# Norms taken per pair of tiles inside the stage that makes x, with roots out of PSUM, hand-over per tile and feed-forwards written out

## The reference

```python
def rmsnorm(x, g):
    return x * rsqrt(mean(x * x, axis=-1) + 1e-6) * g

# first block, layers l = 0, 1
h = rmsnorm(x, norm_mix[l]) * (1 + scale) + shift          # norm n1
proj = h @ w_in[l]                                         # then RWKV-7 and MLA branches, gates, merged
x = x + gate * (merged @ w_o[l])
h = rmsnorm(x, norm_ffn[l]) * (1 + scale) + shift          # norm n2
f = swiglu(h) if l == 0 else moe_swiglu(h)                 # (silu(h @ w1) * (h @ w3)) @ w2; 8 experts, top 2
x = x + gate * f
x = rmsnorm(x, norm_final)                                 # norm nf

# second block, layers l = 0, 1
h = rmsnorm(x, attn_norm[l])                               # norm m1
proj = h @ w_in[l]                                         # two attentions (q and k normed per head), gates
x = x + merged @ w_out[l]
h = rmsnorm(x, ffn_norm[l])                                # norm m2
x = x + (silu(h @ w1) * (h @ w3)) @ w2
```

## Time and profile before

| | us |
|---|---|
| median of 3 runs | 3870.16 (3866.35 to 3871.33) |
| profiled execution, its time | 3868.01 |
| its span | 3866.2 |
| PE busy | 3623.4 (94%) |
| DVE busy | 817.5 (21%) |
| ACT busy | 466.5 (12%) |
| granted TensorE clock, mean | 0.957 of full speed |

### The profile page before, as it was taken

The page is one execution under the profiler, slowest core; times in us unless marked ns, Lnnn a source line. Parts: engine busy times, 40 slices in busy tenths (PEclk is TensorE's granted clock), DMA queues, the critical chain, the costliest instruction groups (busy, mean ns, idle before and its releaser), DMA issues.

```text
span 3866.2 us, 40342 instructions
## 1 busy us (share of the span) xinstructions
PE 3623.4 (94%) x17522; PEld 2807.9 (73%) x17522; DVE 817.5 (21%) x1610; ACT 466.5 (12%) x1027; POOL 35.8 (1%) x74
## 2 busy tenths in 40 slices
PE   6998799899779999999999999999897899997899
PEld 4886688788557777776566777777685788785788
DVE  3523300362431000000000000000454100454100
ACT  2211200212211000000000000000113000113000
POOL 3000000000000000000000000000000000000000
PEclk8999999999989999999999999999896999996999
DMA  8354244334113444447888998985241344341342
GB/s 273 126 186 143 77 152 152 109 105 144 66 66 109 152 152 153 152 153 246 287 286 301 298 300 297 300 297 163 87 141 33 115 139 158 102 133 33 120 157 93
DMA packets 505396, 633.67 MB, mean 164 GB/s; under 512 B 13674, under 2 KB 458240, under 8 KB 505104
## 3 DMA queue, kind: packets, MB, share of 16 engines
q1 hardware_dynamic: 501392, 626.07, 49.3%
q10 hardware_dynamic: 1440, 3.93, 0.3%
q0 software_dynamic: 2400, 1.26, 0.1%
HBM read 630.17 MB, written 1.05 MB: 163 GB/s over the span
## 4 chain that ended last, share of the span: by engine, by line
PE 90%; DVE 5%; issue 2%; ACT 1%; SPq 1%; DMA 0%; ACTq 0%; DVEq 0%
PE bank L447 62%; PE accum L447 27%; DVE w L1498 1%; SPq L2126 1%; DVE w L1519 1%; DVE w L1504 1%; PE bank L538 1%; PE bank L643 1%; ACT w L1165 0%; DMA ring<-in_ada_w_dram 0%; DVE sh L1519 0%; ACT w L1130 0%; DVE w L1501 0%; ACT L1130 0%; ACT h L1130 0%
## 5 line engine op out<-in xcount | busy, mean ns | idle before, releaser
L447 PE MATMUL bank<-h,ring 128*128 128x256 f32 (+1 forms) x3712 | 813.2, 382 | 26.0 <-issue 26.0
L447 PEld LDWEIGHTS bank<-h,ring 128*128 128x128 f32 (+1 forms) x3712 | 703.8, 191 | 133.7 <-issue 35.8
L447 PE MATMUL bank<-w,ring 128*128 128x256 f32 x2816 | 620.1, 381 | 15.4 <-DVE w L1498 14.4
L447 PEld LDWEIGHTS bank<-w,ring 128*128 128x128 f32 x2816 | 538.1, 191 | 104.9 <-issue 25.8
L447 PE MATMUL bank<-ring,w 128*128 128x256 f32 (+1 forms) x3136 | 598.7, 380 | 0.0
L447 PEld LDWEIGHTS bank<-ring,w 128*128 128x128 f32 (+1 forms) x3136 | 481.0, 175 | 96.9 <-issue 15.2
L1498 DVE TENSOR_TENSOR sg<-bank,sg 128x256 f32<-128x256 f32 x140 | 59.5, 425 | 1380.3 <-ACT sg L1130 1380.3
L447 PE MATMUL accum<-ring,qa 128*128 128x512 f32 (+1 forms) x784 | 303.3, 596 | 0.0
L447 PE MATMUL bank<-w 128*128 128x128 f32 (+7 forms) x1728 | 245.4, 312 | 47.8 <-ACT w L1165 32.4
L447 PEld LDWEIGHTS bank<-w 128*128 128x128 f32 (+3 forms) x1728 | 200.1, 193 | 92.3 <-issue 78.0
L447 PE MATMUL accum<-w,ring 128*128 128x256 f32 x1056 | 231.8, 379 | 0.0
(11 more groups left out here) (247 smaller groups left out, 1913.1 us busy)
## 6 DMA issues: line engine op xcount, KB each, us to landing
ring<-in_moe_w_dram SPq DMA_DIRECT2D x336, 1024.0 KB, 5.1
ring<-in_w_in_dram SPq DMA_DIRECT2D x76, 1024.0 KB, 5.3
ring<-in_ada_w_dram SPq DMA_DIRECT2D x48, 1024.0 KB, 8.3
ring<-in_w_ffn_in_dram SPq DMA_DIRECT2D x44, 1024.0 KB, 5.3
ring<-in_ffn_w_dram SPq DMA_DIRECT2D x33, 1024.0 KB, 5.4
ring<-in_w_ffn_out_dram SPq DMA_DIRECT2D x22, 1024.0 KB, 5.0
ring<-in_w_o_dram SPq DMA_DIRECT2D x8, 1024.0 KB, 5.2
ring<-in_w_out_dram SPq DMA_DIRECT2D x8, 1024.0 KB, 5.2
```

Source lines behind the costliest of these rows:

```text
L447: ins = nc.tensor.matmul(o, lhsT, rhs, start=start, stop=stop, skip_group_check=skip)
```

## The change

- **Pairs.** ACT squares x two tiles at a time (`square_pair`), as soon as DVE has updated both, while the projection (or the last product down, or `combine`) still makes the later tiles. PE adds each pair to the sum at a set place inside that stage (`norm_sums`): behind tiles 2, 4 and 6 of `w_o` and `w_out`, and the fourth pair behind the last tile. The sum of the n2 and m2 norms lies in `accum`.
- **Roots.** ACT reads the sum in PSUM and takes the root of scale times sum plus epsilon in the same instruction (`root`), in all norms, the small ones too; DVE only waits and takes the reciprocal (`inverse_root`). So the banks with sums are drained by ACT, at the place where the root stands in ACT's program.
- **Hand-over.** `full_norm` forms each tile of h in one DVE instruction (x times gain times reciprocal root). Where there is a shift, ACT adds it (`shift_h`). Each tile signals; the first eight products of the next stage wait tile by tile (`normed_h`).
- **Feed-forwards.** No loops: eleven chunks written out on PE, ACT, DVE and SP. The four products with zeros stand behind the first chunk up. The last product down goes tile by tile (`ffn_last`) and signals per two tiles; the closing product is gone. At the very end the output is turned half by half.

```diff
+            def norm_sums(tag, take=take):
+                place = []
+                def pair(p):
+                    if p == 0:
+                        place.extend(take(tag + (0,)))
+                    t, f = place
+                    pe.wait_ge(squared, next_of("squared"))
+                    for k in (2 * p, 2 * p + 1):
+                        ins = mm(t[:, 0:T], ones[:, :], sq[:, k, :], k == 0, k == KD - 1, last=k == KD - 1)
+                    if p == 3:
+                        ins.then_inc(f, 1)
+                return pair
+            def normed_h(k):
+                pe.wait_ge(h_ready, next_of("h_ready"))
+                return h[:, k, :]
...
                         contract(t[:, 0:T], kt, lambda k: w(k, m * P, m * P + P), lambda k: src[:, k, :]).then_inc(f, 1)
+                        if pair and at in (2, 4, 6):
+                            pair(at // 2 - 1)
                     release.append(s)
+                if pair:
+                    pair(3)
...
+            def ffn_last(key, b, pair):
+                s2, w2 = piece(2)
+                for k in range(2):
+                    pe.wait_ge(*read_out(key + (k,)))
+                for m in range(KD):
+                    for k in range(2):
+                        ins = mm(accum[:, m, :], w2(k, m * P, m * P + P), hid[:, b, k, :], False, k == 1,
                                  last=(k == 1 and m == KD - 1), skip=True)
+                    if m % 2:
+                        ins.then_inc(acc_full, one("acc_full"))
+                    if pair and m > 4 and m % 2:
+                        pair(m // 2 - 2)
+                release.append(s2)
+                for p in (2, 3) if pair else ():
+                    pair(p)
+            def ffn(key, pair):
+                n = FF // FW
                 for i in range(n):
+                    ffn_up(key + (i,), i == 0)
+                    for b in range(0 if i else 4):
+                        mm(accum[:, 2 * b:2 * b + 2, :].rearrange("p m t -> p (m t)"), zeros, con[:, 0:512],
+                           True, False, skip=True)
                     if i:
                         ffn_down(key + (i - 1,), (i - 1) % 2)
-                ffn_down(key + (n - 1,), (n - 1) % 2)
+                ffn_last(key + (n - 1,), (n - 1) % 2, pair)
...
                     if m % 2:
                         ins.then_inc(acc_full, one("acc_full"))
+                    if m in (3, 5, 7):
+                        norm(m // 2 - 1)
+                norm(3)
...
+            def square_pair(p):
+                fn(sq[:, 2 * p:2 * p + 2, :], x[:, 2 * p:2 * p + 2, :], ACT.Square).then_inc(squared, one("squared"))
+            def root(keys, buf, n, eps=0):
+                at = 0
+                for key, w in keys:
+                    act.wait_ge(*full(key))
+                    fn(buf[:, at:at + w, :], psum_of(key)[:, 0:w * T].rearrange("p (j t) -> p j t", t=T), ACT.Sqrt,
+                       scale=1.0 / n, bias=c("eps", eps, eps + 1)).then_inc(reader_of(key), 1)
+                    at += w
+            def shift_h(shifts):
+                for j in range(KD):
+                    act.wait_ge(scaled_h, next_of("scaled_h"))
+                    fn(h[:, j, :], h[:, j, :], ACT.Identity, bias=shifts[:, j:j + 1]).then_inc(h_ready, one("h_ready"))
...
-            def norm_scale(key, dst):
-                mean_square([(key, 1)], rs, D, EPS)
-                tt(dst[:, :, :], x[:, :, :], rs[:, 0:1, :].to_broadcast([P, KD, T]), MUL).then_inc(dve_step, 1)
-                dve.wait_ge(dve_step, stepped())
+            def inverse_root(keys, buf, n):
+                for key in keys:
+                    dve.wait_ge(*read_out(key))
+                V.reciprocal(buf[:, 0:n, :], buf[:, 0:n, :]).then_inc(dve_step, 1)
+                dve.wait_ge(dve_step, stepped())
+            def full_norm(key, dst, gains, done, name):
+                inverse_root([key], rs, 1)
                 for j in range(KD):
+                    ins = stt(dst[:, j, :], x[:, j, :], gains[:, j:j + 1], rs[:, 0, :], MUL, MUL)
+                    if done is not x_ready or j % 2:
+                        ins.then_inc(done, one(name))
...
-                tt(x[:, :, :], x[:, :, :], accum[:, :, :], ADD).then_inc(x_ready, one("x_ready"))
+                for p in range(4):
+                    dve.wait_ge(acc_full, next_of("acc_full"))
+                    tt(x[:, 2 * p:2 * p + 2, :], x[:, 2 * p:2 * p + 2, :], accum[:, 2 * p:2 * p + 2, :], ADD
+                       ).then_inc(x_ready, one("x_ready"))
```

More of the change, by code:

```diff
@@ L588, in ffn @@
-            def ffn(key, trips, per, rest):
-                for b in range(4):
-                    mm(accum[:, 2 * b:2 * b + 2, :].rearrange("p m t -> p (m t)"), zeros, con[:, 0:512],
-                       True, False, skip=True)
-                assert not release
-                slots.start(3 * per // SLOTS), banks.start(2 * per // NB)
-                with pe.Fori(0, trips) as i:
-                    reg[0] = i
-                    ffn_steps(key + ("loop",), per)
-                slots.end(trips), banks.end(trips)
-                if rest:
-                    ffn_steps(key + ("rest",), rest)
-                mm(accum[:, 7, :], zeros, con[:, 0:T], False, True, last=True, skip=True).then_inc(acc_full, one("acc_full"))
+                ffn_last(key + (n - 1,), (n - 1) % 2, pair)
@@ L675, in combine, with experts @@
                 return ins
-            def experts():
+            def experts(norm):
                 for a in range(TT):
@@ L744, in _ @@
                 mod_piece(0, 0, q)
-            sumsq(("n1", 0), [range(KD)])
+            first = norm_sums(("n1", 0))
+            for p in range(4):
+                first(p)
             for q in range(8, 12):
@@ L1002, in _ @@
             mm(t[:, 0:4], ones[0:64, :], small[0:64, 0:4], last=True).then_inc(f, 1)
-            pe.wait_ge(x_ready, next_of("x_ready"))
+            first = norm_sums(("m1", 0))
+            for p in range(4):
+                first(p)
+            next_of("x_ready", 4)
             for l in range(2):
@@ L1048, in between @@
                         head_turns(4)
-                sumsq(("m1", l), [range(KD)])
                 nat, gate, u = 0, 0, 0
@@ L1349, in _ @@
                 attention(("mla", l))
-                act.wait_ge(*read_out(("wo", l, 7)))
-                squares(x[:, :, :], 8)
-                root([("n2", l, 0)], rs[:, 0:1, :])
+                for p in range(4):
+                    act.wait_ge(*read_out(("wo", l, 2 * p)))
+                    act.wait_ge(*read_out(("wo", l, 2 * p + 1)))
+                    square_pair(p)
+                root([(("n2", l, 0), 1)], rs, D)
+                shift_h(mod[:, 0:8])
                 if l == 0:
-                    ffn(("ffn", 0), FF // FW // 4, 4, FF // FW % 4)
+                    ffn(("ffn", 0))
                 else:
@@ L1397, in head_roots @@
                     g, n = HN_GROUPS[i]
-                    root([("hn", l, g, j) for j in range((n + 1) // 2)], rs2[:, 0:n, :])
+                    root([(("hn", l, g, j), min(2, n - 2 * j)) for j in range((n + 1) // 2)], rs2, 64)
                 def between(u):
@@ L1472, in _ @@
                 squares(oB2[:, :, :], 4)
-                root([("yb2", l, 0), ("yb2", l, 1)], rs2[:, 0:4, :])
-                act.wait_ge(*read_out(("wo2", l, 7)))
-                squares(x[:, :, :], 8)
-                root([("m2", l, 0)], rs[:, 0:1, :])
-                ffn(("ffn2", l), FF // FW // 4, 4, FF // FW % 4)
-                act.wait_ge(x_ready, next_of("x_ready"))
-            for a in range(TT):
-                for g in range(2):
+                root([(("yb2", l, 0), 2), (("yb2", l, 1), 2)], rs2, P)
+                for p in range(4):
+                    act.wait_ge(*read_out(("wo2", l, 2 * p)))
+                    act.wait_ge(*read_out(("wo2", l, 2 * p + 1)))
+                    square_pair(p)
+                root([(("m2", l, 0), 1)], rs, D)
+                ffn(("ffn2", l))
+                if l == 0:
+                    x_squares()
+            next_of("x_ready", 4)
+            for g in range(2):
+                for a in range(TT):
                     act.wait_ge(*full(("out", a, g)))
@@ L1759, in _ @@
                     modulation(0, 0)
-                    norm_apply(h, gain, mod[:, 0:8]).then_inc(h_ready, one("h_ready"))
                     dve.wait_ge(sines, next_of("sines"))
@@ L2151, in ffn_pieces, with ffn @@
                 down(n - 1)
-            def ffn(w1, w3, w2, trips, per, rest):
-                slots.start(3 * per // SLOTS)
-                with sp_.Fori(0, trips) as i:
-                    reg[0] = i
-                    ffn_pieces(per, lambda q: w1, lambda q: w3, lambda q: w2, lambda q: i * (per * FW) + q * FW)
-                slots.end(trips)
-                if rest:
-                    ffn_pieces(rest, lambda q: w1, lambda q: w3, lambda q: w2, lambda q: (trips * per + q) * FW)
+            def ffn(w1, w3, w2):
```

(1 more changed line is left out.)

195 lines of the change are left out of this document (77 added, 118 removed).

## The result

| | kernel before | changed kernel |
|---|---|---|
| median of the runs | 3870.7 us | 3809.1 us (3800.3 to 3810.6, 4 runs) |
| ratio | | 0.9838, 95% interval 0.9821 to 0.9855 |
| profiled execution: span | 3866.2 us | 3807.1 us |
| mean granted TensorE clock | 0.957 | 0.962 |

The change makes the kernel 62 us faster (3870.7 to 3809.1). The forecast was 76 (3793, range 3780 to 3808), so the sign and the mechanism hold and the size doesn't: 16 us are missing (17 between the two profiled executions), and the time lies 1 us outside the range. All the places named in the prediction gave something; the question is where the 16 went. Numbers with an x in PE's rows count records, two for a product.

What follows compares the result with a forecast made beforehand. PE, 90% of what ended last, was taken to bound the kernel through its work and waits around norms. Gains of 79.9 less costs of 3.6 took 76.3 from 3868.0, giving 3791.7; median about 3793, range 3780 to 3808.

Steps and rivals of the forecast that it cites:

- The chain of a norm: From the last update of x through square, table load, root and reciprocal to the first tile of h: 4.65 us.
- nf and both m1: Norms nf and m1 of layer 0 together gain 12.3 us; m1 of layer 1 gains 12.3 us.
- n1 of layer 1: Norm n1 in layer 1: 19.15 us becomes 6.9, closing product gone too, a gain of 12.3 us.
- n2 of layer 1: From layer 1's last product of x to the second logits product: 18.1 us becomes 11.8, gain 6.3.
- rival 2: A table load's drain shows where a root follows at once behind a square; 3800 us, chance 6%.
- rival 4: Instruction supply: PE stands in the 33 straight-code feed-forward chunks; at 2.5 us each 3876 us, slower; chance 3%.
- rival 3: The hand-over fails: sums stop the projection or per-tile signals are slow; some 60% of the gain, 3824 us; chance 8%.
- kk: Third tile behind kk's sums waits 2.5 us for a bank ACT drains; net cost taken as 1.1 per layer.
- rival 1: The clock falls everywhere all the same, at n2, n2 and both m2: 10 us more at most, 3803; chance 12%.
- The three restarts: First products of feed-forwards behind n2 of layer 0 and both m2: gains 8.1, 10.5 and 10.5, together 29.1 us.
- 3.6, bounds 0 and 8: Total cost in us: 2.2 for kk's bank waits, 0.4 for doubled roots, 1.0 for hn's bank waits.
- yb2: In both layers the table load runs beside the sums, leaving a root of 0.63: gain 2.45 each, 4.9 us.

Runs made afterwards that it cites:

- before_straight: The kernel before with only its three feed-forward loops written out as straight code; 3871.2 us against 3866.2, ratio 1.0016.
- kk_dve: Changed kernel with kk alone undone: DVE takes its sums out of their banks, ACT takes one root in SBUF; 3813.6 us, ratio to before 0.9850.
- zeros_gap: Changed kernel with the feed-forwards' zeros moved into PE's wait between the norm's sums and the first tile of h; 3794.4 us, ratio to before 0.9814.
- zeros_twice: Changed kernel with the feed-forwards' zeros written in the wait for h and again behind the first chunk up; 3812.6 us, ratio to before 0.9852.
- best2: Changed kernel with zeros in the wait, added products ahead of n1 of layer 1, both m1 and in the attentions, kk's sums in upper banks; 3749.4 us.
- warm_att: Changed kernel with one overwritten product of 512 columns with zeros in a wait inside each attention head; 3776.3 us, ratio to before 0.9755.
- before_warm_att: The kernel before with one added product of 512 columns in each attention head's wait, nothing else; 3843.9 us, ratio 0.9935.
- shift_layer1: Changed kernel with 1.73 us of overwritten products in the second tile of layer 1's first projection; 3812.6 us.
- kk_upper: Changed kernel with the two sums of kk in upper banks that the products behind don't use; 3812.5 us, ratio to before 0.9866.
- h_whole: Changed kernel, but PE waits for all eight tiles of h ahead of each norm's first product; 3824.9 us, ratio to before 0.9881.

## Why the prediction was right, and where it was wrong

- **The chain of a norm** was right: 6.1 measured for 5.6 between the last product and the first of the next stage; the 0.5 are 0.05 to 0.1 more at each of the root, the scaling, the shift and the hand-overs.
- **Sums inside the projections, zeros at 3.45, the end, nf and both m1**: as forecast, to 0.6. n1 of layer 1 gave 1.2 less and n2 of layer 1 1.4 less; some 0.5 of each is the longer chain, and the rest was not taken apart.
- **One sign was off against the prediction's own sum**: it wanted 7 to 9 us between the last product of x and the next stage, while its terms for n2 of layer 0 give 5.6; 6.1 came.
- **Table loads**: the root starts 0.01 behind its load, so rival 2 didn't come. The Trainium skill (ScalarE: Activation LUTs, "What ACT_TABLE_LOAD costs") counts a drain of about 1.38 us with each load of 1.28. This trace doesn't agree: 0.02 stand ahead of the load at 463.26 and 0.01 behind it.
- **The other rivals**: rival 4 didn't come (chunks of 20.72, in before_straight too), nor rival 3.
- **kk**: the wait is 2.48, net 0.8 and 1.1 by kk_dve, about as taken.
- **The step that failed first** is the sentence "I have counted the zeros at full clock and the first products of n1 and m1 as before", with rival 1's 12% for the clock falling all the same. It has no term for the first products of the three feed-forwards, which the sums of n2 and m2 take at full clock. The zeros did escape the lower clock, but these products took their place under it: 4 us at 0.43 a record behind n2. The three restarts gave 20.3 for 29.1. zeros_gap and zeros_twice show that the clock is 2.0 to 2.6 of each, 7.0 of the 8.8 in all; the other 1.8 are mostly the chain's 0.5 three times. Moving the zeros out of the wait, which the prediction counted as a gain of 2.3 each, took the cover off what came next.
- **The step that failed second** is the cost side: "3.6, bounds 0 and 8". It counted waits and instructions and took blocks that the change doesn't touch at their old time. Measured, the first blocks lost 13.4, of which layer 0's attention 5.2, the stretch after 812 in layer 1 4.3 and layer 1's attention 1.3 go with a lower granted clock. The 4.3 come in every profile of a kernel made from the changed one except best2; the 5.2 come in some executions of one program and not in others. The pair warm_att and before_warm_att points the same way (67.6 for 61.6), within the noise.
- **yb2** gave 8.6 for 4.9, the other way round: 3 of it because a low stretch of 7 us behind layer 0's was gone. That is luck, since the prediction had no such term; without it the miss would be some 3 us larger.

What stays open is why a first block's attention has anything from 3 to 31 us at the lower clock. It isn't the time at which it is reached alone (shift_layer1), nor kk's wait (kk_upper and kk_dve, without it, have 31 us in layer 1). In layer 0 it isn't the program either: zeros_gap and the changed kernel are the same up to there, and have 3 and 17. The 4.3 after 812 have no cause shown either: they are in every kernel made from the changed one except best2, which has 3 us there where they have 14.

## What to carry to other kernels

A gain counted in waits is not yet a gain in time where PE's granted clock moves: before summing, list the stretches at the lower clock and ask of each edit what stands behind its new wait, also in stages that it doesn't touch. A short wait in which PE would stand is the best place for work that must be done anyway (the zeros: 13.6 us for moving 22 records), and failing that for products that nobody reads. When an edit's median goes against its mechanism, compare the traces product by product before dropping it: kk_upper and zeros_twice did locally what was expected and lost it elsewhere. And one profile per kernel is not enough to charge a stage to an edit, where the same program has 3 or 17 us at the lower clock in it.

## What was unexpected of the hardware

- One added product of 512 columns in a wait of 0.67 us, in 40 heads, raised the granted clock of the second blocks' attentions from 0.50 and 0.56 to 0.94 and 0.93, and the kernel became 32 us faster.
- Executions of one program differ by 8 us (3801.9 and 3809.7) in step with their mean granted clock (0.965 and 0.961); in warm_att, with most of the low stretches gone, five lie within 1.3.
- Six profiles of one program up to layer 0's attention have 17 us at the lower clock there (four) or 3 us (two), a difference of 5 us.
- Ahead of the first feed-forward a wait of 6.46 (h_whole) and one of 3.67 (changed kernel) were followed by the same loss, 2 to 2.5 us.
